# Moving the running sums of a gated-recurrence scan from one engine to another, with a second pair of scaled operands and two modulation pieces placed elsewhere

## What is computed

```
x <- LN(ALPHA*x + 0.5*gate0*FFN1(x*(1+scale0)+shift0))
x <- LN(ALPHA*x + gate1*W_out[A|B|C|D](x*(1+scale1)+shift1))   # four token mixers side by side
x <- LN(ALPHA*x + 0.5*gate2*FFN2(x*(1+scale2)+shift2))
```

```
att[i,j] = sum_k q[i,k] * key[j,k] * exp(cum[i,k] - cum[j,k])      for j <= i within the chunk
o_intra  = att @ v;   state' = exp(last) * state + sum_j key[j]*exp(last-cum[j]) v[j]
```

## Time and profile before

| | |
|---|---|
| time, median of 3 runs | 3230.68 us (3225.84 to 3233.95) |
| the profiled execution | 3226.51 us, its span 3224.7 us |
| mean granted TensorE clock | 0.963 |
| PE busy | 2998.4 us, 93% of the span |
| DVE, ACT, POOL busy | 1254.8, 913.7, 144.9 us |
| the second scan, levels 0 to 7, first layer | 736.65 to 847.11 us |
| the same, second layer | 2323.92 to 2433.54 us |

### The profile page before, as it was taken

How to read it: one execution, slowest core, us unless ns; L and a number is a source line. 1 busy time by engine, 2 the same in 40 slices (tenths; PEclk the granted TensorE clock), 3 DMA queues, 4 the chain that set the end, 5 groups by cost and what they waited for, 6 DMA issues and landing times.

```text
span 3224.7 us, 46427 instructions
## 1 busy us (share of the span) xinstructions
PE 2998.4 (93%) x20149; PEld 2647.7 (82%) x20149; DVE 1254.8 (39%) x1639; ACT 913.7 (28%) x1270; POOL 144.9 (4%) x88
## 2 busy tenths in 40 slices
PE   6999998997789999999979999989978998999997
PEld 6999997775556589999979999967655665999996
DVE  3223236435443442322542322464363426223226
ACT  3222223322344132222242121233223433221223
POOL 0000000105200000000000000000150000000000
PEclk8999999999889999999989999999987999999998
DMA  8223233104220122222532232421142001223221
GB/s 295 66 67 84 78 106 115 53 27 131 79 86 1 40 78 66 80 78 73 164 106 69 72 83 70 133 71 53 53 157 83 29 1 50 81 59 90 68 67 51
DMA packets 359016, 259.02 MB, mean 80 GB/s; under 512 B 27152, under 2 KB 310100, under 8 KB 358740
## 3 DMA queue, kind: packets, MB, share of 16 engines
q1 hardware_dynamic: 358868, 256.85, 26.4%
HBM read 253.25 MB, written 3.57 MB: 80 GB/s over the span
## 4 chain that ended last, share of the span: by engine, by line
PE 85%; DVE 7%; ACT 3%; DMA 2%; issue 1%; SPq 1%; POOL 0%; DVEq 0%; ACTq 0%; PEldq 0%; POOLq 0%
PE banks L730 54%; PE banks L646 17%; ACT arena L1248 2%; PE banks L597 2%; PE banks L1165 2%; PE banks L845 1%; PE banks L1186 1%; DVE x_res L1805 1%; PE banks L1016 1%; DMA w_slots<-in_w_mod 1%; PE banks L1158 1%; DMA w_slots<-in_ffn_w_down 1%; DVE w_split L1684 1%; PE banks L911 1%; PE banks L896 1%
## 5 line engine op out<-in xcount | busy, mean ns | idle before, releaser
L730 PE MATMUL banks<-h_hi,w_split 128*128 128x320 f32 x5376 | 1184.5, 309 | 1.0 <-DVE mod L1633 1.0
L730 PEld LDWEIGHTS banks<-h_hi,w_split 128*128 128x128 f32 x5376 | 899.2, 188 | 1.4 <-issue 1.4
L730 PE MATMUL banks<-h_lo,w_split 128*128 128x320 f32 x2688 | 830.6, 309 | 0.0
L730 PE MATMUL banks<-hid_hi,w_split 128*128 128x320 f32 x2816 | 625.1, 310 | 0.1
L1684 DVE TENSOR_TENSOR w_split<-w_slots,w_split 128x2048 fp32r<-128x2048 f32 x152 | 348.4, 2292 | 424.0 <-ACT w_split L1248 423.9
L730 PEld LDWEIGHTS banks<-h_lo,w_split 128*128 128x128 f32 x2688 | 504.6, 188 | 0.0
L1248 ACT ACTIVATE arena<-banks 128x640 f32<-128x640 f32 (+8 forms) x336 | 169.4, 535 | 1082.0 <-PE banks L730 804.2
L730 PEld LDWEIGHTS banks<-hid_hi,w_split 128*128 128x128 f32 x2816 | 472.8, 188 | 2.0 <-issue 1.6
L730 PE MATMUL banks<-hid_lo,w_split 128*128 128x320 f32 x1408 | 435.5, 309 | 0.0
L1248 ACT ACTIVATE w_split<-w_slots 128x2048 fp32r<-128x2048 f32 x152 | 290.1, 1909 | 407.2 <-PE banks L730 371.2
L1748 DVE TENSOR_TENSOR arena<-arena,banks 128x640 f32<-128x640 f32 x88 | 72.2, 821 | 767.5 <-ACT arena L1248 767.5
(11 more groups left out here) (260 smaller groups left out, 2643.1 us busy)
## 6 DMA issues: line engine op xcount, KB each, us to landing
w_slots<-in_ffn_w_gu SPq DMA_DIRECT2D x176, 512.0 KB, 5.1
w_slots<-in_ffn_w_down SPq DMA_DIRECT2D x64, 384.0 KB, 3.7
w_slots<-in_w_mod SPq DMA_DIRECT2D x12, 2048.0 KB, 7.9
arena<-in_w_mod SPq DMA_DIRECT2D x10, 2048.0 KB, 12.9
w_slots<-in_ffn_w_down SPq DMA_DIRECT2D x64, 320.0 KB, 4.3
h_mod<-in_w_mod SPq DMA_DIRECT2D x8, 2048.0 KB, 8.1
mixed<-in_w_mod SPq DMA_DIRECT2D x6, 2048.0 KB, 9.7
w_slots<-in_w_in SPq DMA_DIRECT2D x6, 2048.0 KB, 8.4
```

The costliest lines, as they stand in the source:

```text
L730: ins = mm(banks[:, b0 + hf, 0:HALF], w[:, k, :], x[:, k, t], start=w is wlo and k == 0, stop=w is whi and x is hi and k == kt - 1, skip_g ...
```

## The change

- The four adds of a level move from POOL to DVE and stand in front of the products of the same level. DVE's merge of a level now comes after the adds and the products of the next level.
- `QL` and `KL` exist twice, by the parity of the level. ACT's exponentials of level `lev` wait for the products of the levels up to `lev - 2` only.
- Four pieces (10, 11, 13, 15) are computed in the scan, in levels 0, 2, 4 and 6. Pieces 16 and 17 are computed in the last feed-forward after its second job, as 4 and 5 are in the first.
- POOL clears `SE` and `PB` first; `SIN` now shares its place with the first pair of `QL` and `KL` and is cleared after level 6.

```diff
-FIRST_MODS, RING_MODS = (0, 2, 1, 3, 4, 5), (10, 11, 13, 15, 16, 17)
+FIRST_MODS, RING_MODS, RING_AT = (0, 2, 1, 3, 4, 5), (10, 11, 13, 15), {0: 10, 2: 11, 4: 13, 6: 15}
+GATE_MODS = {0: (4, 5), 2: (16, 17)}
...
-        QL, KL = view(8960, 2, TOK), view(10240, 2, TOK)
+        QL, KL = ([view(first + i * 1280, 2, TOK) for first in (15360, 8960)] for i in range(2))
...
# SP, feed-forward
                             if sub == 0:
                                 sp.wait_ge(s["f_done"], o["f_done"])
-                                fill_mod(l, 4)
-                                fill_mod(l, 5)
+                            else:
+                                sp.wait_ge(mod_row, mod_at[l, 14] + 1)
+                            for i in GATE_MODS[sub]:
+                                fill_mod(l, i)
...
# PE, feed-forward
-                            if sub == 0:
-                                pe.wait_ge(f_freed[0], o["f_freed"][0] + 1)
-                                for i in (4, 5):
-                                    mod_piece(l, i, 2)
...
+                            pe.wait_ge(f_freed[0], o["f_freed"][0] + n0 // 2 + 1)
+                            for i in GATE_MODS[sub]:
+                                mod_piece(l, i, 2)
+                            for i in GATE_MODS[sub]:
+                                mod_turn(l, i, 3)
+                            pe.wait_ge(mod_done, mod_at[l, GATE_MODS[sub][1]] + 1)
...
# PE, scan
-                    q, k = (QL if lev else Q), KL
+                    q, k = (QL[lev % 2] if lev else Q), KL[lev % 2]
...
-                    if 1 <= lev <= len(RING_MODS):
-                        i = RING_MODS[lev - 1]
+                    if lev in RING_AT:
+                        i = RING_AT[lev]
...
# ACT, scan
-                    act.wait_ge(s["att_done"], o["att_done"] + lev * NCH)
                     if lev > 1:
+                        act.wait_ge(s["att_done"], o["att_done"] + (lev - 1) * NCH)
                         act.wait_ge(s["sums"], o["sums"] + 4 * (lev - 1))
...
-                    if lev >= 2:
-                        mod_copy(l, RING_MODS[lev - 2], 6)
+                    if lev - 1 in RING_AT:
+                        mod_copy(l, RING_AT[lev - 1], 6)
...
# DVE, scan
-                merge(0)
                 for lev in range(1, LEVELS + 1):
                     m = 2 ** (lev - 1)
+                    wide = [P, 2 * TOK // (2 * m), m]
                     dve.wait_ge(s["exps"], o["exps"] + 4 * lev)
-                    v.tensor_tensor(QL, QL, Q, ALU.mult).then_inc(s["prods"], 1)
-                    (k1, k2) = halves(KL, m)
+                    (p1, p2), (i1, i2), (e1, _), (_, b2) = (halves(x, m) for x in (PF, SI, SE, PB))
+                    for i, (dst, add) in enumerate(((e1, p2[:, :, m - 1:m]), (b2, i1[:, :, 0:1]), (p2, p1[:, :, m - 1:m]), (i1, i2[:, :, 0:1]))):
+                        if i >= 2:
+                            dve.wait_ge(s["sums"], o["sums"] + 4 * (lev - 1) + i - 1)
+                        v.tensor_tensor(dst, dst, bc(add, wide), ALU.add).then_inc(s["sums"], 1)
+                    ql = QL[lev % 2]
+                    v.tensor_tensor(ql, ql, Q, ALU.mult).then_inc(s["prods"], 1)
+                    (k1, k2) = halves(KL[lev % 2], m)
                     v.tensor_tensor(k1, k1, halves(KF, m)[0], ALU.mult).then_inc(s["prods"], 1)
                     v.tensor_tensor(k2, k2, halves(KB, m)[1], ALU.mult).then_inc(s["prods"], 1)
-                    if lev >= 2:
-                        mod_add(l, RING_MODS[lev - 2], 7)
-                    merge(lev)
+                    merge(lev - 1)
+                    if lev - 1 in RING_AT:
+                        mod_add(l, RING_AT[lev - 1], 7)
+                merge(LEVELS)
...
# POOL, scan
-                link(g.memset(SIN, 0.0))
-                pool.sem_inc(s["sin_zero"], 1)
                 link(g.memset(SE, 0.0))
                 link(g.memset(PB, 0.0))
                 pool.sem_inc(s["excl_zero"], 1)
-                pool.wait_ge(s["gla_act"], o["gla_act"] + 1)
-                for lev in range(1, LEVELS + 1):
...
-                        g.tensor_tensor(dst, dst, wide(add), ALU.add).then_inc(s["sums"], 1)
-                        pool.wait_ge(s["sums"], o["sums"] + 4 * (lev - 1) + i + 1)
+                pool.wait_ge(s["att_done"], o["att_done"] + LEVELS * NCH)
+                link(g.memset(SIN, 0.0))
+                pool.sem_inc(s["sin_zero"], 1)
```

More of the change, by code:

```diff
@@ L266, in trunk_kernel @@
         for l in range(DEPTH):
-            MOD_AT[l, 4], MOD_AT[l, 5] = arena[:, FG * TOK - SLOT:FG * TOK], arena[:, 2 * FG * TOK - SLOT:2 * FG * TOK]
+            for pair in GATE_MODS.values():
+                for n, i in enumerate(pair):
+                    MOD_AT[l, i] = arena[:, (n + 1) * FG * TOK - SLOT:(n + 1) * FG * TOK]
             for pair in (ffn_mods(l, 0), norm_mods(l, 0), ffn_mods(l, 2), norm_mods(l, 2)):
@@ L1022, in _ @@
                             weights(fill)
[L1023 to L1024 removed]
+                        for x in sorted(RING_AT):
+                            if x < lev:
+                                pe.wait_ge(mod_done, mod_at[l, RING_AT[x]] + 1)
                         side(name, w_slot(fill, 8, 256 if fill == "a" else 512), c0, P)
@@ L1332, in ffn @@
                         pairs = HIDHI[:, 0:FG - 1].rearrange("p (i c) t -> p i c t", c=2)
-                        early = sub == 0 and g == 0
-                        if early:
+                        if g == 0:
                             for c in range(2):
-                                gate(c, c, c, c, pairs[:, 0:1, c, :], lambda: weights_hi(c + 2))
+                                gate(c, c, n0 + c, h0 + c, pairs[:, 0:1, c, :], lambda: weights_hi(n0 + c + 2))
                                 if c == 0:
-                                    mod_copy(l, 4, 2)
-                                    mod_copy(l, 5, 2)
-                        with act.Fori(1 if early else 0, FG // 2) as i:
+                                    for i in GATE_MODS[sub]:
+                                        mod_copy(l, i, 2)
+                        with act.Fori(1 if g == 0 else 0, FG // 2) as i:
                             for c in range(2):
@@ L1759, in ffn @@
                         hi2, lo2 = (x[:, 0:FG - 1].rearrange("p (i c) t -> p i c t", c=2) for x in (HIDHI, HIDLO))
-                        early = sub == 0 and g == 0
-                        if early:
+                        if g == 0:
                             for c in range(2):
-                                hidden(c, c, c, hi2[:, 0:1, c, :], lo2[:, 0:1, c, :], lambda: weights_lo(c + 2))
+                                hidden(c, c, h0 + c, hi2[:, 0:1, c, :], lo2[:, 0:1, c, :], lambda: weights_lo(n0 + c + 2))
                                 if c == 0:
-                                    mod_add(l, 4, 3)
-                                    mod_add(l, 5, 3)
-                        with dve.Fori(1 if early else 0, FG // 2) as i:
+                                    for i in GATE_MODS[sub]:
+                                        mod_add(l, i, 3)
+                        with dve.Fori(1 if g == 0 else 0, FG // 2) as i:
                             for c in range(2):
@@ L1996, in _ @@
                     dve.wait_ge(p_freed[p], o["p_freed"][p] + len(FIRST_JOBS[p::2]))
-                finish(v.tensor_tensor(KL, KF, KB, ALU.add), "level_k", 1)
+                finish(v.tensor_tensor(KL[0], KF, KB, ALU.add), "level_k", 1)
                 def merge(lev):
```

16 lines of the change are left out of this document (3 added, 13 removed).

## The result

The changed kernel takes 3324.97 us (median of 4 runs, 3323.19 to 3325.57) against 3232.02 us (4 runs, 3225.84 to 3233.95) before: ratio 1.030, 95% interval 1.028 to 1.032. It is slower, and 3 us from the 3328 that was forecast.

A forecast was written before the change was run, and what follows sets the result against it. PE, busy 93% of the span, was taken as the bound; in the scan the new order makes a serial chain. 3226.5 + 85.8 (scans) + 11.6 (pieces 16, 17) = 3323.9, as a median 3328 us, range 3298 to 3345.

The forecast's parts named there:

- Point 1: Scan: PE does three chunks of a level, then stands 7 to 10 us until the late merge on DVE begins.
- Point 2: Scan: ACT's exponentials of level n+2 queue behind level n's side-product copy-out; with the PE stops, +42.9 us a layer.
- The adds on DVE: Scan: four strided, broadcast adds a level at 0.82 us each, starts 0.75 apart, 3.05 us together.
- The cold side products: Scan: side products of levels 0, 1, 3, 5 begin after idle time at lower clock, 10.6 us each.
- Point 3: Last feed-forwards: pieces 16 and 17 cost PE 5.8 us each time, +11.6 us in all.
- rival of the late tile: Last feed-forwards: the tile behind pieces 16 and 17 comes late, up to 2 x 10 us, 3348 us; chance 0.06.
- The waits for pieces: Scan: PE's waits for piece transfers go, 4.63 us for one of three pieces; counted inside the sum.
- Point 4: Scan: POOL's clear of SIN starts after level 6, needs some 2.4 us, its reader comes 15 us later: no cost.
- Adds and products of 2.12 us even without POOL: Scan rival: DVE's strided adds and products stay at 2.12 us each, +109 us, 3437 us; chance 0.05.
- PE stays the bound: Scan rival: levels close up, 31 us less a layer, 3180 us, faster than before; chance 0.05.
- E + S + P: Scan, per level: ACT's exponentials (2.65 us), DVE's adds (3.05) and products (3.0); with the merge's start 11.4 us.
- All warm: Scan case without PE's cold starts: +27.6 us a layer, +55 in all, given as 3301 us.

The follow-up runs named there:

- e1_merge_first: Changed kernel with DVE's merge of a level moved ahead of the next level's adds and products: 3224.88 us.
- e8_merge_between: Changed kernel with DVE's merge of a level moved ahead of the next level's products but still behind its adds: 3279.86 us.
- e2_exps_early: Changed kernel with ACT's exponentials moved ahead of the copy-out of the side product and of the copy of a piece's rows: 3250.80 us.
- e3_both: Changed kernel with the edits of e1_merge_first and e2_exps_early together: 3227.15 us.
- e5_pieces_alone: Kernel before with only the modulation pieces moved as in the change; adds, merge, exponentials and single QL and KL as before: 3212.64 us.
- e5b_pieces_alone: The same kernel as e5_pieces_alone, timed again with more rounds: 3213.00 us.
- e4_products_first: Changed kernel with DVE doing merge, products, then adds; ACT's exponentials ahead of the side product's copy-out but behind the copy of a piece's rows: 3199.27 us.
- e6_adds_on_pool: Changed kernel with the four adds of each level back on POOL, all else as changed: 3315.87 us.
- e7_products_first_pool: The kernel of e4_products_first with the adds on POOL: 3198.69 us.

## Why the prediction was right, and where it was not

The forecast was right, and the mechanism was the one that was found; that the sum came within 3 us is in part luck, as said below. The table has the forecast times T(n) (all five chunks of level n done) beside those of the changed kernel, which started its scan 1.5 us later (738.13 against 736.65).

| | T(0) | T(1) | T(2) | T(3) | T(4) | T(5) | T(6) | transposes |
|---|---|---|---|---|---|---|---|---|
| predicted | 749.8 | 775.0 | 797.8 | 813.0 | 835.8 | 851.0 | 873.8 | 890.0 |
| measured, less 1.5 | 749.5 | 774.2 | 796.0 | 811.5 | 833.4 | 848.7 | 870.8 | 886.7 |

- **Point 1, PE stops with three chunks done: right.** Seven waits for L2007, 7.25 and 7.94 us in the rows above, in every level from 0 to 6. The runs e1_merge_first and e8_merge_between, in which nothing but the merge moves, show that its place causes them.
- **Point 2, the exponentials behind the copy-out: right.** The exponentials at 786.11 follow the copy-out of 785.46, and e2_exps_early, which alone undoes it, takes 74 us away. The prediction didn't say that the two links are one loop, which either cut opens; e2_exps_early, e1_merge_first and e3_both together show it.
- **The adds on DVE: right, at the low end.** The groups of DVE by form (count, busy us, mean ns), to be read beside the 2121 and 819 ns of the earlier trace rows:

```profile
L2018 DVE TENSOR_TENSOR arena<-arena 128x640 f32<-128x640 f32 x56 | 42.4, 820 | 96.8 <-ACT arena L1253 96.8
...
L2022 DVE TENSOR_TENSOR arena<-arena 128x640 f32<-128x640 f32 x14 | 11.4, 816 | 0.0
```

  Strides and broadcasts cost nothing here: 820 ns against 819. With starts 0.74 apart the four take 3.03 us (taken: 3.05).
- **The cold side products: mis-sized.** I took 10.6 us from the earlier trace rows; the one at 775.74 takes 9.68, and with the other three it is 9.7 to 10.1. Levels with a side product are 21.8 to 22.1 us instead of 22.8, those with a piece alone 15.3 to 15.5 instead of 15.2, level 0 to 1 24.7 instead of 25.2. The scan thus grew by 39.6 and 40.4 us and not by 42.9: **80.0 instead of 85.8**.
- **What lies behind the scan: left out.** 1.6 and 3.6 us more there, in the first layer at a granted clock of 0.79 in its first 80 us where before had 0.83 and 0.87. That is no more than one kernel varies by (4.4 and 3.3 us between e5_pieces_alone and e5b_pieces_alone), so it can't be laid to the change. Another 1.7 us stand at the start of the kernel; it is 1.6 in e5b_pieces_alone and 0.0 in e3_both, so it isn't the change's either. These 6.9 us about cancel the 5.8 too many in the scans: the sum is better than its terms, and that is luck.
- **Point 3, pieces 16 and 17: right.** PE's stretch without L735 is 5.8 us in both layers, as taken; the last feed-forwards as a whole grew by 5.8 and 4.9, and why the second grew less stays open. The timeline of PE in the last feed-forward of the first layer, beside the earlier trace rows:

```profile
1210.34 1.95 PE L602 MATMUL banks<-arena,cond 128*32 128x128 f32 x64
...
1216.18 0.41 PE L735 MATMUL banks<-h_hi,w_split 128*128 128x320 f32 x1 [0.54 <-DVE mod L1637]
```

  5.84 us, with no wait for the transfer. The tile of job 2 isn't late: ACT splits it at 1196.96, 27.6 us behind the end of the mixers' LayerNorm (1169.34), where before it was 29.0. The rival of the late tile did not come.
- **The waits for pieces: right** that they go. What the prediction missed is how much that part is worth alone. It stood inside the sum and nowhere by itself; e5b_pieces_alone gives 12 us to it net, hidden in the changed kernel by 105 to 112 us of order.
- **Point 4, POOL: right**, its clear of SIN starts at 872.41 and takes 2.23 us, 16 us ahead of the transposes.
- **The rivals.** Adds and products of 2.12 us even without POOL are out by the rows above (820 and 816 ns). "PE stays the bound" (3180) was to decide at some 6 us for E + S + P and the start of the merge; e4_products_first, which takes adds and merge out of that sum, comes nearest to it: 3199.
- **Slips in the sums.** All warm is 3297.4 (3328 less 2 x 15.3), not 3301, and 3328 plus 13 is 3341, not 3345. The sum gives the scan 153.4 us (110.5 + 42.9), while the list of signs says 150; 150.0 was measured. None of these decides anything.

## What to carry to other kernels

When PE takes its result banks in turn, the instruction that frees a bank belongs ahead of all that prepares the next step, in its own engine's queue; here one line's place was worth 100 us of 3225. For each queue, write down who waits for each entry and how soon, and place the entry that opens a loop first. A double buffer brings little while its writer still stands behind another wait: with ACT's order as it was, the scan is 98.8 us with two pairs of QL and KL and the adds on DVE (e1_merge_first) and 100.2 with one pair and the adds on POOL (e5b_pieces_alone). No run has the second pair alone. And of a change with several parts, time each alone, since some 12 us of gain were hidden here under more than 100 of loss.

## What the runs showed of the hardware

- **Who starts first decides what DVE pays beside POOL.** DVE's product of 1280 columns took 1.49 us when it started 0.11 us ahead of POOL's first add (e6_adds_on_pool) and 2.43 us when POOL was already at work (e7_products_first_pool); all 12 such products of e6_adds_on_pool that start 0.11 us ahead take 1.49, and the two that start 0.02 us behind POOL take 3.13; the 640 columns behind it took 2.15 to 2.44 beside POOL and 0.82 without. POOL's four adds took 8.53 us beside DVE's products and 5.59 away from them. The Trainium skill, page "SBUF — State Buffer", section "Who interferes with whom", says that a VectorE instruction with two SBUF inputs contends with a GpSimd one that reads SBUF; these rows agree. The prediction has the two shut each other out for a whole instruction, which that section says of VectorE's two-port modes; the ends in e6_adds_on_pool fit it here too: DVE's product ended at 770.49, POOL's first add (3.05 us) at 772.16, DVE's key product (2.44 us) at 772.84. Why it is then no loss to leave the adds on POOL is a matter of when they run, not of their price.
- **A stage whose code no edit touched varied by 12 us.** From the transposes to the end of the mixers the profiled executions took 276.3 to 288.6 us, with granted clocks of 0.57 to 0.91 in stretches of 40 us. The runs of one kernel scatter with the mean clock too: the 12 of e5b_pieces_alone go from 3211.81 us at 0.964 to 3220.16 at 0.961. The same kernel as e5_pieces_alone took 280.7 and 279.6 us there, at 0.74 in the first 40 us, where e5b_pieces_alone took 276.3 at 0.91. This stage is where e1_merge_first, whose scan is 1.5 us a layer shorter than that of e5b_pieces_alone, loses to it (by 4.9 and 8.4 us; the medians are 12 us apart). What brings the clock of this stage down in one execution and not in another stays open; no run here isolates it.
